# A two-layer hybrid encoder on one core: the order of the first query products, the first loads in halves, and the place of the probabilities' division

## The chip, the cores and the metric

The kernel runs on one core of a Trainium2 chip. The metric is the device time of one execution in microseconds (us). A core has four compute engines that run side by side and meet only at semaphores: TensorE (PE: matrix products; its weight loads are shown apart as PEld), VectorE (DVE), ScalarE (ACT) and GpSimd (POOL), and SyncE (SP), which here issues the loads. Each engine takes its instructions in the order in which they are written, so an instruction that waits holds up all that stand behind it on its engine.

## The reference

The input x has 256 tokens of width 1024. It is normalised once, then passes through two layers:

```
h = layer_norm(x, ln_in_g, ln_in_b)
for i in range(DEPTH):                                   # DEPTH = 2
    z = h @ w_in[i]
    q, k, v, xr, yr, ga, gr = jnp.split(z, split_points, axis=-1)
    ...                                                  # rotary on q, k
    attn = local_attention(q, k, v, attn_sink[i])        # softmax with a sink, 8 heads, 2 kv heads
    ...                                                  # hr: two directions of conv + gated recurrence
    rnn = hr * jax.nn.gelu(yr)
    merged = (jax.nn.sigmoid(ga) * (attn @ w_proj_attn[i])
              + jax.nn.sigmoid(gr) * (rnn @ w_proj_rnn[i]))
    h = layer_norm(DN_ALPHA * h + merged @ w_out[i], ln1_g[i], ln1_b[i])
    ...                                                  # gated MLP with a width-3 conv, per-layer embedding
    h = layer_norm(DN_ALPHA * h + ffn + ple, ln2_g[i], ln2_b[i])
```

All is float32.

## The kernel before

**Three products for one.** TensorE multiplies in a rounded float32 (fp32r). To keep precision each operand is split into a high part (the rounded value) and a low part (what is left), and a product is made of three: high by high, high by low, low by high (the helper three, L522 to L526). The high part of a weight is cast by ScalarE (split_hi, L846 to L850), its low part is made by VectorE as raw minus high (split_lo, L1157 to L1162). The normalised input x is turned by TensorE (turn_rows, L684) into PSUM (misc), from there ScalarE writes x_hi (L864) and VectorE x_lo (L1281), for each tile t of 128 tokens and each half c of the 1024 features.

**Items and homes.** All weights are cut into 168 items of at most 1 MB (ITEMS). An item is loaded by SP into a home: five ordinary ones (W_SLOTS) and two that are buffers of other stages at other times (STATE_HOME, RNN_HOME). The table at L140 to L151 gives each item the home that was used longest ago; where a home had a former item, SP waits until TensorE has used that one (load_item, L450). ScalarE and VectorE split ahead: split_to(l, name, part) splits every item up to the named one plus three.

**The start.** SP loads tile 0 of x, item 0 (first half of the rows of q0), the gains and offsets of the norm (lnp, 1 MB since it is broadcast to all partitions), items 1 and 2, then two small arrays and further items; ScalarE issues the load of tile 1 of x and of the rotary table once tile 0 is there (L1032 to L1034). VectorE takes the statistics of a tile (L1178), the inverse root in small steps (L1188 to L1200), then for each half two passes over 512 columns (L1204, L1207); both passes wait for the whole of lnp (L1201). TensorE turns each half when its norm is done, and begins the query units: q0 and q1 are the 1024 query columns in two units of 512; a unit has two halves hh of the rows, and for every half and token tile token_part (L534) makes 12 products of 512 columns, the three kinds interleaved row block by row block. So the first product waits for the low part of item 0 (s_split, L531) and for x_lo.

**The block loop.** After q0, q1 and xr0 come eight rounds i (WITH_BLOCK, L771): half of a unit of the input projection, one block of the recurrence's gates (gates_block), the other half, and in rounds 3 to 6 turn_probs of attention round r = i - 3, in rounds 2 to 5 the scores of round i - 2. ScalarE makes the exponentials, VectorE the maximum (softmax_max) and the division by the sum (softmax_norm, L1360), whose result turn_probs waits for; it also waits for attn_ready(r), the low part of the attention output of the round before (attn_out, L1367).

## Time and profile before

| | us |
|---|---|
| median of 3 runs | 957.37 (957.37 to 957.76) |
| the profiled execution, its own time | 957.63 |
| its span, first to last instruction | 955.8 |
| TensorE busy | 930.9 (97%) |
| VectorE busy | 725.6 (76%) |
| ScalarE busy | 577.1 (60%) |

All rows below come from the profiled execution. Times are counted from the start of its span. In a timeline a row holds start, duration, engine, line, operation, what it writes and reads, and, in brackets, how long the engine had idled before and what ended that.

### The profile page before, as it was taken

The page shows a single profiled execution, that of the slowest core. Times are in us where ns is not written, and L with a number is a line of the kernel's source. Part 1 is how long each engine was busy: PE and PEld are TensorE (multiplying, and loading weights), DVE is VectorE, ACT ScalarE, POOL GpSimd, SP SyncE. Part 2 cuts the span into 40 slices and gives each one's busy share as a digit, 9 for nine tenths or more (in the row PEclk, how much of TensorE's full clock was granted, in tenths as well). Part 3 has the DMA queues.
Part 4 walks back from the last instruction along what each step waited for, and adds up shares of the span by engine and source line. Part 5 has one row for each costly group of instructions (what it writes and reads, how often), then busy time and mean ns, then how long its engine had stood idle before and what let it go on. Part 6 is the DMA issues. An engine that isn't in the chain of part 4 may idle for free.

```text
span 955.8 us, 12485 instructions
## 1 busy us (share of the span) xinstructions
PE 930.9 (97%) x5068; PEld 801.6 (84%) x5068; DVE 725.6 (76%) x971; ACT 577.1 (60%) x729; POOL 1.5 (0%) x9
## 2 busy tenths in 40 slices
PE   4999999999999999999999999999999999999996
PEld 3898888888888888888889988888888888888885
DVE  6768798697868876867867688887878686866855
ACT  3478889954356654546335889987535555645540
POOL 0000000000000000000000000000000000000000
PEclk9999999999999999999999999999999999999999
DMA  8456435575576556555453645445746755655621
GB/s 312 154 170 204 136 111 164 191 258 204 184 228 203 186 180 203 190 178 197 166 187 113 216 142 174 133 156 196 275 141 219 257 176 187 205 180 185 207 93 44
DMA packets 118040, 174.61 MB, mean 183 GB/s; under 512 B 3936, under 2 KB 78944, under 8 KB 117344
## 3 DMA queue, kind: packets, MB, share of 16 engines
q1 hardware_dynamic: 117696, 173.27, 54.5%
q8 instruction: 40, 0.66, 0.3%
q10 hardware_dynamic: 288, 0.56, 0.2%
q14 instruction: 16, 0.13, 0.0%
HBM read 172.76 MB, written 1.05 MB: 182 GB/s over the span
## 4 chain that ended last, share of the span: by engine, by line
PE 83%; DVE 8%; ACT 7%; issue 1%; DMA 1%; SPq 0%; DVEq 0%; ACTq 0%
PE ring L524 13%; PE ring L526 13%; PE ring L525 13%; PE ring L577 9%; PE ring L573 9%; PE ring L576 5%; PE ring L574 5%; PE misc L524 4%; PE misc L525 4%; PE misc L526 4%; DVE sb_w_lo L1161 2%; ACT sb_w_hi L850 2%; PE misc L682 2%; DVE sb_tmp L1381 1%; ACT sb_soft L943 1%
## 5 line engine op out<-in xcount | busy, mean ns | idle before, releaser
L1161 DVE TENSOR_TENSOR sb_w_lo<-sb_raw,sb_w_hi 128x2048 fp32r<-128x2048 f32 (+1 forms) x140 | 299.6, 2151 | 72.4 <-ACT sb_w_hi L850 72.3
L850 ACT CAST sb_w_hi<-sb_raw 128x2048 fp32r<-128x2048 f32 (+1 forms) x140 | 249.8, 1795 | 19.9 <-DMA sb_raw<-in_w_in_dram 5.0
L524 PE MATMUL ring<-sb_w_hi,sb_x_both 128*128 128x512 f32 x304 | 121.9, 401 | 2.1 <-DVE sb_x_both L1281 2.1
L526 PE MATMUL ring<-sb_w_hi,sb_x_both 128*128 128x512 f32 x304 | 119.4, 393 | 0.0
L525 PE MATMUL ring<-sb_w_lo,sb_x_both 128*128 128x512 f32 x304 | 119.4, 393 | 0.0
L577 PE MATMUL ring<-sb_x_both,sb_w_hi 128*128 128x512 f32 x272 | 107.6, 396 | 0.0
L573 PE MATMUL ring<-sb_x_both,sb_w_hi 128*128 128x512 f32 x272 | 107.5, 395 | 0.0
L576 PE MATMUL ring<-sb_x_both,sb_w_lo 128*128 128x256 f32 x272 | 75.7, 278 | 0.0
L574 PE MATMUL ring<-sb_x_both,sb_w_lo 128*128 128x256 f32 x272 | 75.4, 277 | 0.0
L524 PE MATMUL ring<-sb_x_both,sb_w_hi 128*128 128x256 f32 x256 | 73.0, 285 | 0.0
L525 PE MATMUL ring<-sb_x_both,sb_w_hi 128*128 128x256 f32 x256 | 72.4, 283 | 0.0
L526 PE MATMUL ring<-sb_x_both,sb_w_lo 128*128 128x256 f32 x256 | 72.4, 283 | 0.0
L524 PEld LDWEIGHTS ring<-sb_w_hi,sb_x_both 128*128 128x128 f32 x304 | 57.8, 190 | 14.1 <-DVE sb_x_both L1281 2.7
L526 PEld LDWEIGHTS ring<-sb_w_hi,sb_x_both 128*128 128x128 f32 x304 | 57.6, 190 | 12.5
L525 PEld LDWEIGHTS ring<-sb_w_lo,sb_x_both 128*128 128x128 f32 x304 | 57.9, 190 | 11.4
L968 ACT COPY sb_soft<-ring 128x512 f32<-128x512 f32 x24 | 14.1, 587 | 84.5 <-PE ring L577 84.5
L576 PEld LDWEIGHTS ring<-sb_x_both,sb_w_lo 128*128 128x128 f32 x272 | 51.0, 188 | 12.4
L574 PEld LDWEIGHTS ring<-sb_x_both,sb_w_lo 128*128 128x128 f32 x272 | 51.1, 188 | 11.7
L524 PE MATMUL misc<-sb_w_hi,sb_a_hi 128*128 128x512 f32 x140 | 54.7, 390 | 0.0
L526 PE MATMUL misc<-sb_w_hi,sb_a_lo 128*128 128x512 f32 x140 | 54.5, 389 | 0.0
L525 PE MATMUL misc<-sb_w_lo,sb_a_hi 128*128 128x512 f32 x140 | 54.5, 389 | 0.0
L864 ACT ACTIVATE sb_x_both<-misc 128x512 fp32r<-128x512 f32 x24 | 13.9, 596 | 65.0 <-PE misc L682 65.0
(210 smaller groups left out, 2070.3 us busy)
## 6 DMA issues: line engine op xcount, KB each, us to landing
sb_raw<-in_w_in_dram SPq DMA_DIRECT2D x42, 1024.0 KB, 5.2
sb_raw<-in_w_up_dram SPq DMA_DIRECT2D x34, 1024.0 KB, 5.2
sb_raw<-in_w_down_dram SPq DMA_DIRECT2D x18, 1024.0 KB, 4.9
sb_raw<-in_w_proj_attn_dram SPq DMA_DIRECT2D x8, 1024.0 KB, 5.1
sb_raw<-in_w_proj_rnn_dram SPq DMA_DIRECT2D x8, 1024.0 KB, 5.1
sb_hb<-in_w_up_dram SPq DMA_DIRECT2D x8, 1024.0 KB, 5.3
sb_raw<-in_w_out_dram SPq DMA_DIRECT2D x6, 1024.0 KB, 5.6
sb_raw<-in_w_ple_gate_dram SPq DMA_DIRECT2D x6, 1024.0 KB, 5.6
```

The source lines that it names most:

```text
L524: nc.tensor.matmul(dst, lhs[0], rhs[0], start=first, stop=False)
L525: nc.tensor.matmul(dst, lhs[0], rhs[1], start=False, stop=False)
L526: return nc.tensor.matmul(dst, lhs[1], rhs[0], start=False, stop=last)
L573: nc.tensor.matmul(bank_of(*key), hi[:, cols], x_both[:, k], start=k == 0, stop=False)
L574: nc.tensor.matmul(bank_of(*key)[:, 0:SEQ], lo[:, cols], x_hi[:, k], start=False, stop=False)
L576: nc.tensor.matmul(bank_of(*key)[:, 0:SEQ], lo[:, cols], x_hi[:, k + 1], start=False, stop=False)
L577: last = nc.tensor.matmul(bank_of(*key), hi[:, cols], x_both[:, k + 1], start=False, stop=k + 2 == KT)
L682: return nc.tensor.transpose(dst, src, ident[:])
L850: nc.scalar.copy(hi_at[home][:, 0:size], raw_at[home][:, 0:size]).then_inc(s_hi_part, 1)
L864: nc.scalar.activation(x_hi[:, 4 * c:4 * c + 4, t * P:(t + 1) * P], misc[:, 2 * t + c, :].rearrange("p (k t) -> p k t", k=4), ACT.Copy, sc ...
L968: nc.scalar.copy(half_of(name)[:, hh], ring[:, pair:pair + 2, SEQ:2 * SEQ]).then_inc(s_taken, 1)
L1161: nc.vector.tensor_tensor(lo_at[home][:, 0:size], raw_at[home][:, 0:size], hi_at[home][:, 0:size].bitcast(F32), ALU.subtract).then_inc(s_s ...
```

## The change

It has four parts. (1) In layer 0 the 96 query products are reordered: the 64 whose weight operand is a high part come first, with the turns of x between them, and the 32 with a low part last (first_query_units); layer 1 keeps its order. VectorE no longer splits items 0 and 1 before the norm of tile 1. (2) The first loads: gains and offsets in two halves of 512 columns ahead of the weights, item 0 in two halves with a semaphore each, tile 1 of x issued by SP after them, the rotary table by ScalarE later; ScalarE casts item 0 in two halves. (3) The home table prefers the two shared homes for the first items, so items 0 and 1 lie there, items 2 to 6 in the ordinary ones. Evaluated by hand, the table leaves every FORMER from item 7 on as it was; items 5 and 6, which had to wait for items 0 and 1, wait for nothing. (4) In the block loop of both layers VectorE's softmax_norm moves from behind the gates weight's low part to directly behind the first half's, ahead of attn_out and conv_lo; softmax_max of rounds 1 to 3 moves to the end of the round before, ahead of that round's scan.

```diff
--- before.py
+++ after.py
@@ -140,7 +140,7 @@
 HOME, FORMER, LOADED = [], [], []
 _latest, _loads = {}, [0] * HOMES
 for _n, (_l, _name, _part) in enumerate(ITEMS):
-    _home = min(homes_of(_n), key=lambda home: _latest.get(home, home - HOMES))
+    _home = min(homes_of(_n), key=lambda home: _latest.get(home, home - HOMES * (1 + (home >= W_SLOTS))))
     _former = _latest.get(_home)
     if _home >= W_SLOTS and _n > ITEM[_l, "xr0", 0] and (_former is None or _former < ITEM[_l, "xr0", 0]):
         _former = "state" if _home == STATE_HOME else "rnn"
@@ -153,7 +153,8 @@
 
 def in_pe_order(l):
 
-    steps = [("q0", 0), ("q0", "half"), ("q0", 1), ("q1", "half"), ("q1", 0), ("q1", 1), ("xr0", 0), ("xr0", 1)]
+    steps = [("q0", 0), ("q0", "half"), ("q0", 1)] if l else [("q0", "half"), ("q0", 0), ("q0", 1)]
+    steps += [("q1", "half"), ("q1", 0), ("q1", 1), ("xr0", 0), ("xr0", 1)]
     for i, name in enumerate(WITH_BLOCK):
         feature = UNITS[name][0] == "feature"
         steps += [(name, 0 if feature else "half")]
@@ -471,11 +475,24 @@
                     sp.wait_ge(s_rnn_ready, value("rnn_ready", l, 2))
                 sp.dma_start(lnp[:], a["ln"][bass.ds(2 * l + n, 1)].to_broadcast((P, 2, D))).then_inc(s_lnp, 16)
 
+            def load_first_norm(c, signal):
+
+                at = slice(512 * c, 512 * c + 512)
+                sp.dma_start(lnp[:, :, at], a["ln"][0:1, :, at].to_broadcast((P, 2, 512))).then_inc(signal, 16)
+
             sp.dma_start(h[:, 0, :], a["x"][0, 0:P, :]).then_inc(s_h[0], 16)
+            load_first_norm(0, s_lnp_left)
+            load_first_norm(1, s_lnp)
             for l in range(DEPTH):
                 head = ITEM[l, "q0", 0]
-                load_item(head)
-                load_norm(l, 0)
+                if l == 0:
+                    for i, signal in enumerate((s_raw_first, s_raw[HOME[0]])):
+                        dst = raw_at[HOME[0]][:, 1024 * i:1024 * i + 1024].rearrange("p (k n) -> p k n", k=2)
+                        sp.dma_start(dst, item_source(0)[0][:, 2 * i:2 * i + 2]).then_inc(signal, 16)
+                    sp.dma_start(h[:, 1, :], a["x"][0, P:SEQ, :]).then_inc(s_h[1], 16)
+                else:
+                    load_item(head)
+                    load_norm(l, 0)
                 for n in range(head + 1, head + 3):
                     load_item(n)
                 sp.wait_ge(s_rnn_ready, value("rnn_ready", l, 0))
@@ -678,6 +695,78 @@
                         if (t, c) == (1, 0) and l + 1 < DEPTH:
                             turn_h(l + 1, 0, 0, [1])
 
+            def high_pass(l, name, hh, t, ready, x, ks=range(4)):
+
+                n = ITEM[l, name, hh]
+                hi = hi_at[HOME[n]]
+                if n == 0 and ks[-1] < 2:
+                    pe.wait_ge(s_hi_first, 1)
+                else:
+                    pe.wait_ge(s_hi_part, n + 1)
+                first = hh == 0 and x is x_hi and ks[0] == 0
+                if first:
+                    pe.wait_ge(s_emptied[RING[l, name, t][0]], free(l, name, t))
+                if x is x_hi:
+                    pe.wait_ge(s_x_hi, value("x_hi", l, ready))
+                else:
+                    x_ready(l, ready)
+                for k in ks:
+                    nc.tensor.matmul(bank_of(l, name, t), x[:, 4 * hh + k, t * P:(t + 1) * P],
+                                     hi[:, 512 * k:512 * k + 512], start=first and k == ks[0], stop=False)
+
+            def high_passes(l, name, hh, t, ready):
+                high_pass(l, name, hh, t, ready, x_hi)
+                high_pass(l, name, hh, t, ready, x_lo)
+
+            def low_pass(l, name, hh, t):
+
+                hi, lo = weights(l, name, hh)
+                for k in range(4):
+                    last = nc.tensor.matmul(bank_of(l, name, t), x_hi[:, 4 * hh + k, t * P:(t + 1) * P],
+                                            lo[:, 512 * k:512 * k + 512], start=False, stop=hh == 1 and k == 3)
+                return last
+
+            def first_query_units(l):
+
+                turn_h(l, 0, 0, [0])
+                high_pass(l, "q0", 0, 0, 1, x_hi, range(0, 2))
+                turn_h(l, 0, 0, [1])
+                high_pass(l, "q0", 0, 0, 1, x_lo, range(0, 2))
+                high_pass(l, "q0", 0, 0, 1, x_hi, range(2, 4))
+                high_pass(l, "q0", 0, 0, 1, x_lo, range(2, 4))
+                high_passes(l, "q0", 1, 0, 2)
+                turn_h(l, 0, 1, [0])
+                high_passes(l, "q1", 0, 0, 1)
+                turn_h(l, 0, 1, [1])
+                high_passes(l, "q0", 0, 1, 3)
+                high_passes(l, "q1", 0, 1, 3)
+                high_passes(l, "q0", 1, 1, 4)
+                for t in range(TT):
+                    high_passes(l, "q1", 1, t, 2 + 2 * t)
+                for name in ("q0", "q1"):
+                    low_pass(l, name, 0, 0)
+                    low_pass(l, name, 0, 1).then_inc(s_products, 1)
+                    low_pass(l, name, 1, 0).then_inc(s_products, 1)
+                    low_pass(l, name, 1, 1).then_inc(s_products, 1)
+
...
             def turn(dst, src):
                 return nc.tensor.transpose(dst, src, ident[:])
 
@@ -749,24 +838,9 @@
                 attn = (a_hi, a_lo)
                 rnn = (r_hi, r_lo)
                 if l == 0:
-                    turn_h(l, 0, 0)
-                x_ready(l, 1)
-                token_part(l, "q0", 0, 0, x)
-                x_ready(l, 2)
-                token_part(l, "q0", 1, 0, x).then_inc(s_products, 1)
-                turn_h(l, 0, 1, [0])
-                if l:
-                    token_part(l, "q1", 0, 0, x)
-                turn_h(l, 0, 1, [1])
-                x_ready(l, 3)
-                token_part(l, "q0", 0, 1, x).then_inc(s_products, 1)
-                x_ready(l, 4)
-                token_part(l, "q0", 1, 1, x).then_inc(s_products, 1)
-                if l == 0:
-                    token_part(l, "q1", 0, 0, x)
-                token_part(l, "q1", 0, 1, x).then_inc(s_products, 1)
-                for t in range(TT):
-                    token_part(l, "q1", 1, t, x).then_inc(s_products, 1)
+                    first_query_units(l)
+                else:
+                    query_units(l)
                 feature_unit(l, "xr0")
                 for i, name in enumerate(WITH_BLOCK):
                     half = feature_half if UNITS[name][0] == "feature" else mixer_token_half
@@ -847,7 +921,13 @@
 
                 home, size = HOME[n], item_size(n)
                 act.wait_ge(s_raw[home], LOADED[n])
-                nc.scalar.copy(hi_at[home][:, 0:size], raw_at[home][:, 0:size]).then_inc(s_hi_part, 1)
+                at = slice(1024 if n == 0 else 0, size)
+                nc.scalar.copy(hi_at[home][:, at], raw_at[home][:, at]).then_inc(s_hi_part, 1)
+
+            def split_first_half():
+
+                act.wait_ge(s_raw_first, 16)
+                nc.scalar.copy(hi_at[HOME[0]][:, 0:1024], raw_at[HOME[0]][:, 0:1024]).then_inc(s_hi_first, 1)
 
             split = [0]
 
@@ -1029,16 +1109,20 @@
             def pg_out(l, c, t):
                 out_of(l, f"pg{c}", t, gr[:, t, 512 * c:512 * c + 512], ACT.Tanh, 0.5)
 
-            act.wait_ge(s_h[0], 16)
-            act.dma_start(h[:, 1, :], a["x"][0, P:SEQ, :]).then_inc(s_h[1], 16)
-            act.dma_start(rope[:], a["rope"]).then_inc(s_rope, 16)
             for l in range(DEPTH):
                 if l == 0:
+                    split_first_half()
+                x_parts(l, 0, [(0, 0)], 1.0)
+                if l == 0:
                     split_to(l, "q0", 0, 0)
-                x_parts(l, 0, [(0, 0), (0, 1)], 1.0)
+                x_parts(l, 1, [(0, 1)], 1.0)
                 if l == 0:
                     split_to(l, "q1", 0, 0)
-                x_parts(l, 2, [(1, 0), (1, 1)], 1.0)
+                x_parts(l, 2, [(1, 0)], 1.0)
+                x_parts(l, 3, [(1, 1)], 1.0)
+                if l == 0:
+                    split_to(l, "q1", 1, 0)
+                    act.dma_start(rope[:], a["rope"]).then_inc(s_rope, 16)
                 split_to(l, "q0", 1)
                 unit_out(l, "q0")
                 split_to(l, "q1", 0)
@@ -1198,8 +1282,11 @@
                     norm_step(l, n, t, 5 + 2 * i)
                     nc.vector.scalar_tensor_tensor(out=y, in0=u, scalar=1.5, in1=y, op0=ALU.add,
                                                    op1=ALU.mult).then_inc(s_ln_step, 1)
-                dve.wait_ge(s_lnp, 32 * l + 16 * n + 16)
                 for c in range(2):
+                    if (l, n, t, c) == (0, 0, 0, 0):
+                        dve.wait_ge(s_lnp_left, 16)
+                    else:
+                        dve.wait_ge(s_lnp, 32 * l + 16 * n + 16)
                     at = slice(512 * c, 512 * c + 512)
                     nc.vector.scalar_tensor_tensor(out=h[:, t, at], in0=h[:, t, at], scalar=mean, in1=lnp[:, 0, at],
                                                    op0=ALU.subtract, op1=ALU.mult).then_inc(s_ln_step, 1)
@@ -1506,9 +1593,7 @@
                 add_ffn(l, 0, 1)
                 norm_rest(l, 0, 0)
                 if l == 0:
-                    split_to(l, "q0", 0, 0)
                     x_parts(l, 0, [(0, 0), (0, 1)], 1.0)
-                    split_to(l, "q0", 1, 0)
                     add_ffn(l, 1, 0)
                 else:
                     x_parts(l, 0, [(0, 0)], 1.0)
@@ -1533,22 +1618,20 @@
                 split_to(l, "xr1", 1)
                 conv(l, 2)
                 for i, name in enumerate(WITH_BLOCK[1:], 1):
-                    if 4 <= i <= 6:
-                        softmax_max(l, i - 3)
                     split_to(l, name, 0)
+                    if 3 <= i <= 6:
+                        softmax_norm(l, i - 3)
                     if i >= 4:
                         attn_out(l, i - 4)
                     if i + 1 < 2 * RNN_BLOCKS:
                         conv_lo(l, i + 1)
                     split_to(l, f"rg{i // RNN_BLOCKS}", i % RNN_BLOCKS)
-                    if 3 <= i <= 6:
-                        softmax_norm(l, i - 3)
                     gate_input(l, i)
                     split_to(l, name, 1)
                     if i + 2 < 2 * RNN_BLOCKS:
                         conv(l, i + 2)
-                    if i == 2:
-                        softmax_max(l, 0)
+                    if 2 <= i <= 5:
+                        softmax_max(l, i - 2)
                     if name == "kv":
                         rotate(l)
                     if i % 2 == 1:
```

## Rows read from the trace of the kernel before

**Rows 1.** The page, its parts on busy time and on slices.

```profile
PE 930.9 (97%) x5068; PEld 801.6 (84%) x5068; DVE 725.6 (76%) x971; ACT 577.1 (60%) x729; POOL 1.5 (0%) x9
...
PEclk9999999999999999999999999999999999999999
```

**Rows 2.** Waits of TensorE, whole span: total us, times, longest.

```profile
PE misc L682 <- DVE sb_h L1207: 12.5, 3, 11.8
PE misc L682 <- DVE sb_soft L1360: 2.8, 4, 1.1
```

**Rows 3.** Chain that ended last, first 45 us: start, us, what.

```profile
1.64 8.47 DMA sb_lnp<-in_ln_dram
...
15.99 0.79 PE ring L524
...
21.05 0.43 PE ring L526
...
21.85 0.23 PE ring L525
```

**Rows 4.** Timeline of the start, until x_hi of the first half.

```profile
4.30 1.29 DVE L1178 BATCH_NORM_STATS2 sb_st<-sb_h 128x6 f32<-128x512 f32 x2 [4.30 <-DMA sb_h<-in_x_dram]
...
7.00 1.90 ACT L850 CAST sb_w_hi<-sb_raw 128x2048 fp32r<-128x2048 f32 x1 [0.52 <-DMA sb_raw<-in_w_in_dram]
...
10.14 0.75 DVE L1204 SCALAR_TENSOR_TENSOR sb_h<-sb_h,sb_mv,sb_lnp 128x512 f32<-128x512 f32 x1 [2.59 <-DMA sb_lnp<-in_ln_dram]
...
11.83 1.09 PE L682 MATMUL misc<-sb_ident,sb_h 128*128 128x128 f32 x4 [11.83 <-DVE sb_h L1207]
...
12.95 0.60 ACT L864 ACTIVATE sb_x_both<-misc 128x512 fp32r<-128x512 f32 x1 [4.05 <-PE misc L682]
```

**Rows 5.** Bytes moved, 40 slices of the first 50 us.

```profile
GB/s 0 121 342 395 433 439 419 393 371 376 393 385 241 205 401 392 361 265 28 0 0 0 0 0 110 379 372 360 346 115 39 322 68 0 0 179 376 282 2 31
```

**Rows 6.** Timeline, norm of tile 1 and the last turn of x.

```profile
18.96 1.28 DVE L1178 BATCH_NORM_STATS2 sb_st<-sb_h 128x6 f32<-128x512 f32 x2
...
22.91 0.75 DVE L1207 SCALAR_TENSOR_TENSOR sb_h<-sb_h,sb_mv,sb_lnp 128x512 f32<-128x512 f32 x1
...
25.17 0.66 PE L682 MATMUL misc<-sb_ident,sb_h 128*128 128x128 f32 x4 [0.38 <-DVE sb_h L1207]
...
26.21 0.50 PE L524 MATMUL ring<-sb_w_hi,sb_x_both 128*128 128x512 f32 x1 [0.38 <-DVE sb_x_both L1281]
```

**Rows 7.** Timeline, TensorE's first product of xr0 (256 columns).

```profile
42.66 0.28 PE L524 MATMUL ring<-sb_x_both,sb_w_hi 128*128 128x256 f32 x1
```

**Rows 8.** Timeline of VectorE behind the query stage.

```profile
36.61 0.18 DVE L1300 TENSOR_SCALAR sb_lam_t<-sb_lam_t 128x16 f32<-128x16 f32 x1 [2.40 <-ACT sb_lam_t L1047]
...
50.42 2.46 DVE L1381 SCALAR_TENSOR_TENSOR sb_tmp<-sb_xT,sb_rnnp,sb_tmp 128x255 f32<-128x255 f32 x6 [4.77 <-ACT sb_tmp L883]
```

**Rows 9.** Timeline of TensorE at turn_probs, rounds 4 and 6, layer 0.

```profile
132.55 0.28 PE L526 MATMUL ring<-sb_x_both,sb_w_lo 128*128 128x256 f32 x1
133.88 1.09 PE L682 MATMUL misc<-sb_ident,sb_soft 128*128 128x128 f32 x8 [1.05 <-DVE sb_soft L1360]
...
170.64 1.09 PE L682 MATMUL misc<-sb_ident,sb_soft 128*128 128x128 f32 x8 [0.32 <-DVE sb_soft L1360]
```

**Rows 10.** Timeline of VectorE in round 4, layer 0.

```profile
127.50 2.29 DVE L1161 TENSOR_TENSOR sb_w_lo<-sb_raw,sb_w_hi 128x2048 fp32r<-128x2048 f32 x1
129.70 0.68 DVE L1367 TENSOR_TENSOR sb_a_lo<-misc,sb_a_hi 128x512 fp32r<-128x512 f32 x1
...
132.28 0.15 DVE L1355 TENSOR_TENSOR sb_sm<-sb_sm 128x4 f32<-128x4 f32 x1
...
132.68 1.14 DVE L1360 TENSOR_SCALAR sb_soft<-sb_soft,sb_sm 128x256 f32<-128x256 f32 x4
```

**Rows 11.** Timeline of ScalarE, exponentials of round 4.

```profile
127.62 0.47 ACT L943 ACTIVATE sb_soft<-misc,sb_sm 128x256 f32<-128x256 f32 x1 [1.65 <-DVE sb_sm L1351]
...
129.43 0.21 ACT L946 ACTIVATE sb_sm<-sb_sm 128x4 f32<-128x4 f32 x1
```

More of the change, by code:

```diff
@@ L387, in hybrid_encoder @@
         s_lnp = sem("lnp_loaded")
+        s_lnp_left = sem("first_lnp_left_loaded")
+        s_raw_first = sem("first_raw_half_loaded")
+        s_hi_first = sem("first_hi_half")
         s_small = sem("rnn_params_loaded")
```

16 lines of the change are left out of this document (added).

## The prediction

> **What bounds the kernel now.** I read the page first: TensorE is busy 97% of the span, the next engine 76% [rows 1], so a gain has to come out of TensorE's idle time (955.8 - 930.9 = 24.9 us) or out of products that it makes slowly. The list of waits says where that time is: 12.5 us at the start, nearly all of it before the first turn of x, and 2.8 us in four waits of turn_probs for the division of the probabilities [rows 2]. The few us of the last norm's tail are untouched by this change. The chain of waits then names what ends last at the start: the load of gains and offsets, 8.47 us, and only then norm, turn, low parts and the first product at 15.99 [rows 3]. The timeline shows that VectorE had the inverse root ready and stood idle 2.59 us for that load, until 10.14 [rows 4]. 
>
> Tile 0 of x is still the first load, so the statistics start at 4.30 and the root is ready at 10.14 - 2.59 = 7.55 [rows 4]. Gains and offsets now come second: with x 1.05 MB must have come for the left half, 1.57 MB for the right. The bytes moved (1.25 us a slice) add up to 1.07 MB at 5.0 us and 1.6 MB at 6.2 us [rows 5]. Landings lag that sum: item 0 (1.57 MB in order) was cast at 7.00 [rows 4], 0.8 late. So left lands by about 5.8, right by 7.0, both in time. The wait of 2.59 us goes; the first half's norm ends 2.56 earlier and its turn starts at 11.83 - 2.56 = 9.27, ends at 10.36 [rows 4].
>
> What is late next? The left half of item 0 is now fourth: 2.10 MB, moved by 7.4, landed by 8.2, cast (half of 1.90) by 9.2. It is done before x_hi is wanted at 10.4, with 1.2 to spare. x_hi takes 0.60 and ends at 11.0 [rows 4]. The first product no longer needs a low part of a weight nor x_lo, so it starts at about 11.05 instead of 15.99 [rows 3].
>
> That start is not the gain, since VectorE's norm of tile 1 sets the next point. TensorE makes two products (0.59 for the first up to its successor, 0.43), then the turn of the right half (1.09), which ends at 13.15. x_hi of that half ends at 13.8, x_lo on VectorE at 14.4. Only then do VectorE's statistics of tile 1 start, at 14.4 instead of 18.96 [rows 6]: the two low parts that lay ahead (2.20 each, the pitch of a low part is 129.70 - 127.50 [rows 10]) are moved behind. From the statistics to the left half's norm it took 22.91 + 0.75 - 18.96 = 4.70, so TensorE can turn it at 19.15. Until then TensorE has the other 14 products of q0 for tile 0: from 13.15, six of them to 15.7, then eight, for which ScalarE must have cast item 1 (13.8 to 15.6, loaded by 4.2 MB, that is 13.5). At the lower level they end at 19.1, at the upper at 17.6. Either way TensorE arrives by the time the norm is done; the slow pace is hidden there.
>
> From 19.15: the turn (0.45 at the upper level), eight products of q1 (1.9 with the dearer first one) to 21.5, the turn of the right half to 22.0. Remaining are 40 high products and 32 low ones, 72. Before, 72 products were likewise left at 26.21, the first product behind the last turn [rows 6]; they ended at 42.66 [rows 7], a pitch of 16.45/72 = 0.2285. Nothing should stop them in the new order: x_hi and x_lo of tile 1 are ready while q1 and q0 run; item 3's cast ends by 24.4; the five low parts follow each other on VectorE from 23.1 at 2.2 each and the last of the four that the low products want is ready at 32, wanted only from 36.5. So xr0 begins at 22.0 + 16.45 = 38.45. **Term 1: 42.66 - 38.45 = 4.2 us.**
>
> Does it last? VectorE has as much work as before with TensorE 4.2 us further on. After the fifth low part (34.2) come the small steps of the recurrence's parameters, with a wait for an exponential on ScalarE: before it came at 36.61, after 2.40 of waiting [rows 8]. ScalarE now reads out q0 only at about 35.3, casts item 5 (1.9) and reaches it at 37.3. The steps took 3.0 (36.61 to the next low part); item 5's low part is ready at 42.5. TensorE wants it after xr0's first half, 48 products of 256 columns at 0.12 (5.8): 44.2. Cover 1.7 us; beyond it each us costs one. Further on VectorE stood idle 4.77 before the first conv [rows 8], which covers the 4.2. The homes cost nothing: no former item changes from item 7 on, and items 5 and 6 come earlier. The later rotary table (0.45 us of ScalarE's queue, behind it the cast of item 4) is read far later. SP issues two instructions more and one from ScalarE, all ahead of items that have more than 1 us of cover but item 2: moved by 15.5, landed by about 16.3, cast by 18.2, wanted at 19.6.
>
> **Part 2: the division.** In round 4 TensorE's last product before turn_probs starts at 132.55 and holds 0.12; the turns start at 133.88 [rows 9]. Lost: 1.21, that is the idle 1.05 and 0.16 of modelled tail. Round 6 by the same rule: 0.32 + 0.16 = 0.48 [rows 9]. The second layer repeats both (four waits in all [rows 2]). After the change VectorE, free at 129.70 as before (maximum and scan only swap places ahead of 127.50), makes the division at once: 1.5 us (132.28 to 133.82 [rows 10]), done at 131.3, before 132.67. Its own need, the exponentials, ended at 129.64 after ScalarE had waited 1.65 for the maximum [rows 11]; with the maximum ahead of the scan (3.6 us) ScalarE starts as soon as it is free, 1.65 earlier, and is done at 128.0. What is late next is attn_out, which turn_probs also wants: 129.70 + 1.5 + 0.7 = 131.9, 0.8 before TensorE. conv_lo and the gates weight's low part come 1.5 later, wanted a round later (more than 10 us). The scan ends 2.3 later; nobody waits for it within 3 us. **Term 2: 2 x (1.21 + 0.48) = 3.4 us.**
>
> **The sum.** 957.63 - 4.2 - 3.4 = 950.0 against the profiled execution. That execution is 0.26 above the median of the runs, so the median should be **949.8**.
>
> **A rule against it.** The trace shows the pace change between 21.05 and 21.85 [rows 3], in the middle of a stretch of products without a gap that began at 15.99. By the Trainium skill, "TensorE: Matmul & The Clock Gate", Part 1 and the section on transposes, the gate watches activity freely running against the kernel, and a transpose does not count as busy in the same way. Turns now lie among the first products; by that rule the rise could come late against the first product. This trace can't tell it.
>
> **Rivals.**
> (a) The upper level comes late. Each 512-column product before it costs 0.43 - 0.23 = 0.20 more, a turn of four about 0.5. Up to 19.15 that is hidden, as shown. If the rise stays at 21.3 as in the trace of before [rows 3], half of 19.15 to 21.3 is lost: 1.1 us, 950.9. The same page is where this would come from. If it came at 23, 1.9 us: 951.7. For it: turns and a short gap lie in the way. Against: before, turns at 11.83 and a gap of some us ahead of 15.99 did not prevent a rise before 21.85 [rows 3, 4]. Chance 0.17.
> (b) Term 2 fails: a wait on attn_out or on the exponentials replaces the one on the division. The margins are 0.8 and 1.7. Time 953.2. Chance 0.08.
> (c) Term 1 fails, since the weights arrive later than the bytes say or VectorE is late at item 5 by 1.7 and more; or the new order does not let TensorE start early at all. Time between 950.9 and 954.0 with term 2 whole, 956 if VectorE's lateness also reaches into the block loop. Chance 0.07.
> (d) Slower than before: the division stands ahead of attn_out, and in rounds 4 to 6 VectorE idles there for exponentials that ScalarE makes only behind its own attn_out copy. Price: each us of idle beyond 0.8 is a us of TensorE in six rounds; it outweighs both terms from 0.8 + 7.6/6 = 2.1 us of idle, and at 3 us of it the time is 949.8 + 6 x 2.2 = 963. Round 4 shows 1.7 us of cover instead. Chance 0.03.
>
> **How the numbers follow.** The forecast has 0.65, alone it spans 948.8 to 950.8 (its landings, gaps and turns are good to 0.5 each way, and the pace may rise a little late). The range reaches over (a) and a part of (c): 948.6 to 952.4. About 0.2% (1.9 us) can be told from no change in this kernel. Faster: 0.94, from the forecast, (a), (b), and 0.04 of (c). Same: 0.03, the rest of (c). Slower: 0.03, (d).
>
> **What would show it.** In the profile after: no wait of VectorE for gains and offsets, first turn at 9.3, first product at 11.1; statistics of tile 1 at 14.4; the last turn of x at 21.5; xr0's first product at 38.5 and no idle TensorE between 22 and there; the pace at 0.23 before 19. Rounds 4 and 6 without a wait of turn_probs, in both layers, the division directly behind a low part and ending 1.3 us before the turns. Wrong would be: x_hi waiting behind a cast of item 0, TensorE waiting at s_split for item 5, or turn_probs waiting for L1367.

## The result and the profile after

| | before | after |
|---|---|---|
| median, us | 957.37 | 950.35 (949.98 to 950.9, 4 runs) |
| ratio after to before | | 0.9927 (0.9915 to 0.994) |
| profiled execution, own time | 957.63 | 949.98 |
| its span | 955.8 | 948.2 |
| TensorE busy / idle in the span | 930.9 / 24.9 | 928.1 / 20.1 |

The change makes the kernel 7.0 us faster by the medians; forecast were 7.6. Between the two profiled executions it is 7.65, since that of before lies 0.26 above its median and that of the changed kernel is the fastest of its four.

The waits of TensorE over the whole span of the changed kernel (total us, times, longest); the two rows that answer to [rows 2] are the first, 9.9 for 12.5, and the one that is missing: turn_probs waits for nothing.

```profile
PE misc L771 <- DVE sb_h L1294: 9.9, 2, 9.5
PE ring L714 <- ACT sb_r_hi L925: 1.6, 1, 1.6
PE ring L714 <- ACT sb_x_both L944: 0.8, 1, 0.8
```

The timeline of its start, cut to the steps that the prediction dated (start, duration, engine, line, operation, output and inputs, idle time before and what ended it). They answer to [rows 4], [rows 6] and [rows 7].

```profile
4.62 1.29 DVE L1262 BATCH_NORM_STATS2 sb_st<-sb_h 128x6 f32<-128x512 f32 x2 [4.62 <-DMA sb_h<-in_x_dram]
...
7.80 0.75 DVE L1291 SCALAR_TENSOR_TENSOR sb_h<-sb_h,sb_mv,sb_lnp 128x512 f32<-128x512 f32 x1
...
9.48 1.09 PE L771 MATMUL misc<-sb_ident,sb_h 128*128 128x128 f32 x4 [9.48 <-DVE sb_h L1294]
9.54 1.05 ACT L930 CAST sb_scan_hi<-sb_hb 128x1024 fp32r<-128x1024 f32 x1 [7.52 <-DMA sb_hb<-in_w_in_dram]
...
11.34 1.19 PE L714 MATMUL ring<-sb_scan_hi,sb_x_both 128*128 128x512 f32 x2 [0.78 <-ACT sb_x_both L944]
...
14.66 1.28 DVE L1262 BATCH_NORM_STATS2 sb_st<-sb_h 128x6 f32<-128x512 f32 x2
14.90 1.90 ACT L925 CAST sb_r_hi<-sb_r_raw 128x2048 fp32r<-128x2048 f32 x1 [0.87 <-DMA sb_r_raw<-in_w_in_dram]
...
16.85 2.11 PE L714 MATMUL ring<-sb_r_hi,sb_x_both 128*128 128x512 f32 x8 [1.59 <-ACT sb_r_hi L925]
...
19.42 0.66 PE L771 MATMUL misc<-sb_ident,sb_h 128*128 128x128 f32 x4 [0.46 <-DVE sb_h L1294]
...
38.56 0.28 PE L541 MATMUL ring<-sb_x_both,sb_w_hi 128*128 128x256 f32 x1
```

VectorE no longer waits for gains and offsets: its pass starts at 7.80, as soon as the root is there. The first product comes at 11.34 (15.99 before), tile 1's turn at 19.42, and xr0 at 38.56 instead of 42.66. That is 4.10 us.

At turn_probs, rounds 4 and 6 of layer 0 (to be held against [rows 9]):

```profile
128.38 0.28 PE L543 MATMUL ring<-sb_x_both,sb_w_lo 128*128 128x256 f32 x1
128.50 1.04 PE L771 MATMUL misc<-sb_ident,sb_soft 128*128 128x128 f32 x8
...
164.52 0.40 PE L543 MATMUL ring<-sb_w_hi,sb_x_both 128*128 128x512 f32 x1
164.76 1.04 PE L771 MATMUL misc<-sb_ident,sb_soft 128*128 128x128 f32 x8
```

The turns follow the last product after 0.12 and 0.24, which is that product's own pace. Held against before, TensorE is ahead by 4.10 at xr0, by 133.88 - 128.50 = 5.38 at round 4 and by 170.64 - 164.76 = 5.88 at round 6. So the start gives 4.10, round 4 gives 1.28, round 6 gives 0.50. In layer 1 round 4 stands at 591.12 in the changed kernel and 598.33 before, 7.21 ahead; round 6 at 627.38 and 635.12, 7.74 ahead. Next to nothing is given back behind: the two spans differ by 7.6.

### The profile page after: what moved, and what is told of

The parts are those of the page before. It is cut to its first block, busy times and chain, and to the rows that moved or that the text cites. A ratio compares the mean times of both kernels' runs of the same rounds, so it can differ in the third digit from the quotient of the medians.

```text
span 948.2 us, 12500 instructions
## 1 busy us (share of the span) xinstructions
PE 928.1 (98%) x5068; PEld 800.5 (84%) x5068; DVE 724.2 (76%) x971; ACT 576.6 (61%) x730; POOL 1.4 (0%) x9
## 3 DMA queue, kind: packets, MB, share of 16 engines
HBM read 172.76 MB, written 1.05 MB: 183 GB/s over the span
## 4 chain that ended last, share of the span: by engine, by line
PE 97%; DVE 1%; DMA 1%; ACT 0%; SPq 0%; issue 0%; DVEq 0%
PE ring L541 16%; PE ring L543 16%; PE ring L542 16%; PE ring L594 9%; PE ring L590 9%; PE ring L593 5%; PE ring L591 5%; PE misc L543 5%; PE misc L541 5%; PE misc L542 4%; PE misc L771 2%; PE misc L809 1%; PE misc L829 1%; PE ring L714 1%; DMA sb_hb<-in_w_in_dram 1%; PE ring L725 1%
## 5 line engine op out<-in xcount | busy, mean ns | idle before, releaser
L1245 DVE TENSOR_TENSOR sb_w_lo<-sb_raw,sb_w_hi 128x2048 fp32r<-128x2048 f32 x138 | 294.7, 2148 | 67.5 <-ACT sb_w_hi L925 67.4
L925 ACT CAST sb_w_hi<-sb_raw 128x2048 fp32r<-128x2048 f32 x138 | 246.2, 1795 | 16.1 <-DMA sb_raw<-in_w_proj_rnn_dram 3.9
L541 PE MATMUL ring<-sb_w_hi,sb_x_both 128*128 128x512 f32 x272 | 108.1, 397 | 0.0
L543 PE MATMUL ring<-sb_w_hi,sb_x_both 128*128 128x512 f32 x272 | 106.1, 390 | 0.0
L542 PE MATMUL ring<-sb_w_lo,sb_x_both 128*128 128x512 f32 x272 | 106.0, 390 | 0.0
L543 PEld LDWEIGHTS ring<-sb_w_hi,sb_x_both 128*128 128x128 f32 x272 | 51.1, 188 | 11.0
L541 PEld LDWEIGHTS ring<-sb_w_hi,sb_x_both 128*128 128x128 f32 x272 | 51.1, 188 | 10.0
L542 PEld LDWEIGHTS ring<-sb_w_lo,sb_x_both 128*128 128x128 f32 x272 | 51.2, 188 | 9.9
L590 PEld LDWEIGHTS ring<-sb_x_both,sb_w_hi 128*128 128x128 f32 x272 | 51.6, 190 | 0.3
```

What stands on the lines that cost most here:

```text
L541: nc.tensor.matmul(dst, lhs[0], rhs[0], start=first, stop=False)
L542: nc.tensor.matmul(dst, lhs[0], rhs[1], start=False, stop=False)
L543: return nc.tensor.matmul(dst, lhs[1], rhs[0], start=False, stop=last)
L590: nc.tensor.matmul(bank_of(*key), hi[:, cols], x_both[:, k], start=k == 0, stop=False)
L925: nc.scalar.copy(hi_at[home][:, at], raw_at[home][:, at]).then_inc(s_hi_part, 1)
L1245: nc.vector.tensor_tensor(lo_at[home][:, 0:size], raw_at[home][:, 0:size], hi_at[home][:, 0:size].bitcast(F32), ALU.subtract).then_inc(s_s ...
```

## The experiments

Times below are medians; the kernel before, timed beside each of them, took 957.3 to 957.5. Differences from the changed kernel are taken to its 950.35, whose four runs spread over 0.9 us, so a difference of less than about half a us says nothing by itself; there the traces decide.

### Do the two terms add?

**softmax_only**: the kernel before with the block loop's reordering alone.

```diff
                 for i, name in enumerate(WITH_BLOCK[1:], 1):
-                    if 4 <= i <= 6:
-                        softmax_max(l, i - 3)
                     split_to(l, name, 0)
+                    if 3 <= i <= 6:
+                        softmax_norm(l, i - 3)
                     if i >= 4:
                         attn_out(l, i - 4)
...
-                    if 3 <= i <= 6:
-                        softmax_norm(l, i - 3)
                     gate_input(l, i)
...
-                    if i == 2:
-                        softmax_max(l, 0)
+                    if 2 <= i <= 5:
+                        softmax_max(l, i - 2)
```

> The kernel before with the reordering of maximum and division alone. My theory (two terms that add): turn_probs of rounds 4 and 6 no longer waits in either layer, 3.4 us gained, about 954.0. Rival (the term belongs to the change's start, by which engines meet differently, or a wait on attn_out takes its place): under 1 us gained, 956.5 to 957.4.

Measured: 953.71 (ratio 0.9961, 0.9946 to 0.9976), 3.8 us faster than before. No wait of turn_probs is left. **start_only** is the changed kernel with that same diff undone, so it holds the start and the homes.

> The changed kernel with the old places of maximum and division. Two terms that add: 4.1 us gained, about 953.3, xr0's first product at 38.6, and the four waits of turn_probs back with 1.05 and 0.33 of idle. Rival (shifted engines would have hidden those waits anyway, or the start's gain is given back in the block loop): 950.5 or 955 and more.

Measured: 953.8 (0.9965, 0.9952 to 0.9978), 3.7 us faster than before; the four waits are back:

```profile
PE misc L771 <- DVE sb_soft L1447: 2.7, 4, 1.0
```

3.8 and 3.7 make 7.5, the whole change 7.0: the terms add within what the intervals allow. Its profiled execution took 955.39, its other four 953.77 to 954.02; what happened in it is told below, under the pace.

### Which of the two moves in the block loop?

**division_only**: the changed kernel with the maximum of rounds 1 to 3 back behind the scan.

```diff
                 for i, name in enumerate(WITH_BLOCK[1:], 1):
+                    if 4 <= i <= 6:
+                        softmax_max(l, i - 3)
                     split_to(l, name, 0)
...
-                    if 2 <= i <= 5:
-                        softmax_max(l, i - 2)
+                    if i == 2:
+                        softmax_max(l, 0)
```

> The changed kernel with the division at its new place and the maximum of rounds 1 to 3 back behind the scan. My theory: in round 4 the exponentials end about as VectorE gets to the division, so the division's place is enough: at most 0.5 us slower than the whole change, 950.3 to 950.8. Rival (the earlier maximum is needed, else VectorE idles for the exponentials and attn_out, 0.8 of margin, is late): round 4 or 6 waits by 0.5 or more, 951.5 to 953.

Measured: 950.43 (950.08 to 950.83), the changed kernel's time, and no wait of turn_probs. **maximum_only** leaves the maximum at its new place and puts the division back:

```diff
                     split_to(l, name, 0)
-                    if 3 <= i <= 6:
-                        softmax_norm(l, i - 3)
                     if i >= 4:
...
                     split_to(l, f"rg{i // RNN_BLOCKS}", i % RNN_BLOCKS)
+                    if 3 <= i <= 6:
+                        softmax_norm(l, i - 3)
                     gate_input(l, i)
```

> The changed kernel with the maximum at its new place and the division back behind the gates weight's low part. My theory: the division starts no earlier than before, since VectorE's work ahead of it is the same, so the waits of turn_probs stay: 953.3. Rival (the chain was maximum, exponentials, division, and the maximum opens it): 951 or less.

Measured: 953.23, 2.9 slower than the change. Round 4 of layer 0, from TensorE's timeline:

```profile
129.64 1.09 PE L771 MATMUL misc<-sb_ident,sb_soft 128*128 128x128 f32 x8 [0.80 <-DVE sb_soft L1447]
```

The wait is 0.80 where it was 1.05, and in round 6, where start_only waits 0.31, the list of waits has none any more (two waits, 1.6 us in all, for four and 2.7). From turn to turn TensorE still loses 1.0 in round 4 and 0.3 in round 6 of either layer, where start_only loses 1.2 to 1.3 and 0.5. So the expectation had the time, but its reason, a division that starts no earlier, holds only in the main: alone, the earlier maximum takes some 0.2 us at each of the four turns (953.23 against start_only's 953.8). The division's place takes all of the wait, and beside it the maximum's place is worth nothing (division_only).

### The start: which part carries it?

**loads_only**: the kernel before with the new order of its first loads (item 0 in one piece) and nothing else.

```diff
             sp.dma_start(h[:, 0, :], a["x"][0, 0:P, :]).then_inc(s_h[0], 16)
+            for c, signal in ((0, s_lnp_left), (1, s_lnp)):
+                at = slice(512 * c, 512 * c + 512)
+                sp.dma_start(lnp[:, :, at], a["ln"][0:1, :, at].to_broadcast((P, 2, 512))).then_inc(signal, 16)
...
                 load_item(head)
-                load_norm(l, 0)
+                if l == 0:
+                    sp.dma_start(h[:, 1, :], a["x"][0, P:SEQ, :]).then_inc(s_h[1], 16)
+                else:
+                    load_norm(l, 0)
...
-            act.dma_start(h[:, 1, :], a["x"][0, P:SEQ, :]).then_inc(s_h[1], 16)
...
-                dve.wait_ge(s_lnp, 32 * l + 16 * n + 16)
                 for c in range(2):
+                    if (l, n, t, c) == (0, 0, 0, 0):
+                        dve.wait_ge(s_lnp_left, 16)
+                    else:
+                        dve.wait_ge(s_lnp, 32 * l + 16 * n + 16)
```

> The kernel before with the gains in halves as the first load behind tile 0 of x, item 0 in one piece after them and tile 1 of x then, but the products, the low parts of items 0 and 1 and the places of maximum and division as before. If the order of the loads made the start's gain alone: xr0 at 38.6 and 953.3. My theory, that it needs the products' order too: the norm starts 2.3 earlier, but item 0 lands at about 11.3 and its cast and low part end at 13.2 and 15.4, so the first product starts no earlier than 15.5 to 16.5: 956.6 to 957.9, that is same as before.

Measured: 957.82 (ratio 1.0005, 0.9996 to 1.0014), the same as before. Its timeline shows why:

```profile
9.57 1.09 PE L689 MATMUL misc<-sb_ident,sb_h 128*128 128x128 f32 x4 [9.57 <-DVE sb_h L1216]
...
11.16 1.90 ACT L857 CAST sb_w_hi<-sb_raw 128x2048 fp32r<-128x2048 f32 x1 [4.75 <-DMA sb_raw<-in_w_in_dram]
...
13.10 2.29 DVE L1167 TENSOR_TENSOR sb_w_lo<-sb_raw,sb_w_hi 128x2048 fp32r<-128x2048 f32 x1 [2.22 <-ACT sb_w_hi L857]
...
16.04 0.79 PE L531 MATMUL ring<-sb_w_hi,sb_x_both 128*128 128x512 f32 x1 [4.00 <-DVE sb_x_both L1290]
```

The turn comes 2.3 earlier, but item 0's cast and low part now end at 13.1 and 15.3, and the first product stands at 16.04 (15.99 before [rows 3]). The weight has become what the norm was.

**weights_before_gains**: the changed kernel with item 0 (in halves) loaded ahead of gains and offsets.

```diff
             sp.dma_start(h[:, 0, :], a["x"][0, 0:P, :]).then_inc(s_h[0], 16)
-            load_first_norm(0, s_lnp_left)
-            load_first_norm(1, s_lnp)
...
                         sp.dma_start(dst, item_source(0)[0][:, 2 * i:2 * i + 2]).then_inc(signal, 16)
+                    load_first_norm(0, s_lnp_left)
+                    load_first_norm(1, s_lnp)
```

> The changed kernel with item 0 loaded ahead of gains and offsets, as before (all still in halves). Theory A (the order of the first bytes carries the start): the gains' left half lands at about 8.5 to 9 and the right at 10 to 10.5, the norm of the left half starts 1 to 1.5 us later, the right half's waits too, xr0 at 39.8 to 40.3, 951.5 to 952. Theory B (landings of parts overlap so that their order does not matter, and the reordered products alone make the gain): 950.3 to 950.6.

Measured: 951.82, 1.5 slower than the change; first turn at 10.95, tile 1's turn at 20.89, xr0 at 40.05. Theory A. So of the 4.1 us some 1.5 belong to the loads' order once the products are reordered, and none without that.

**item0_whole**: the changed kernel with item 0 loaded and cast in one piece.

```diff
                 if l == 0:
-                    for i, signal in enumerate((s_raw_first, s_raw[HOME[0]])):
-                        dst = raw_at[HOME[0]][:, 1024 * i:1024 * i + 1024].rearrange("p (k n) -> p k n", k=2)
-                        sp.dma_start(dst, item_source(0)[0][:, 2 * i:2 * i + 2]).then_inc(signal, 16)
+                    load_item(head)
...
                 if l == 0:
-                    split_first_half()
+                    split_to(l, "q0", 0, 0)
                 x_parts(l, 0, [(0, 0)], 1.0)
```

> The changed kernel with item 0 loaded and cast in one piece. Theory A (the halves matter through ScalarE's order): item 0 lands at about 10.9, its cast of 1.9 ends at 12.8 and x_hi waits behind it, the first product comes 2 us later, x_lo of the right half and with it the statistics of tile 1 some 2 us later, xr0 at 40.5, about 952.2. Theory B (the halves are hidden by the wait for tile 1): 950.3 to 950.6.

Measured: 952.02, 1.7 slower. From its timeline:

```profile
11.28 1.90 ACT L920 CAST sb_scan_hi<-sb_hb 128x2048 fp32r<-128x2048 f32 x1 [9.26 <-DMA sb_hb<-in_w_in_dram]
13.09 0.59 ACT L939 ACTIVATE sb_x_both<-misc 128x512 fp32r<-128x512 f32 x1
...
13.82 1.19 PE L709 MATMUL ring<-sb_scan_hi,sb_x_both 128*128 128x512 f32 x2 [3.21 <-ACT sb_x_both L939]
```

x_hi stands behind the whole cast on ScalarE, and everything up to xr0 (41.03) is 2.5 later (its profiled execution, 952.28, is 2.3 slower than that of the changed kernel). Theory A.

**old_homes**: the changed kernel with the old table of homes.

```diff
-    _home = min(homes_of(_n), key=lambda home: _latest.get(home, home - HOMES * (1 + (home >= W_SLOTS))))
+    _home = min(homes_of(_n), key=lambda home: _latest.get(home, home - HOMES))
```

> The changed kernel with the old table of homes, so that items 5 and 6 wait again for the last products of items 0 and 1, which the new order makes late (about 32.6 and 34.5). The prediction costed the homes at nothing, seen as an edit to the kernel before. Theory A (nothing here either): 950.3. Theory B (in the new order they carry weight: item 5 lands at about 37.5, ScalarE's cast of it stands ahead of the exponential of the parameters, VectorE's low part of item 5 comes at about 45.5 to 46, and TensorE waits for it 1.5 to 3 us behind xr0's first half): 952 to 953.5.

Measured: 951.72, 1.4 slower. xr0's first product still stands at 38.62; the loss comes behind it:

```profile
38.44 1.90 ACT L925 CAST sb_w_hi<-sb_raw 128x2048 fp32r<-128x2048 f32 x1 [2.65 <-DMA sb_raw<-in_w_in_dram]
40.24 0.21 ACT L1131 ACTIVATE sb_lam_t<-sb_lam_t 128x16 f32<-128x16 f32 x1
40.49 0.17 DVE L1387 TENSOR_SCALAR sb_lam_t<-sb_lam_t 128x16 f32<-128x16 f32 x1 [5.27 <-ACT sb_lam_t L1131]
...
43.37 5.62 DVE L1245 TENSOR_TENSOR sb_w_lo<-sb_raw,sb_w_hi 128x2048 fp32r<-128x2048 f32 x3
...
45.71 0.39 PE L541 MATMUL ring<-sb_x_both,sb_w_hi 128*128 128x256 f32 x1 [1.18 <-DVE sb_w_lo L1245]
```

Item 5 lands at 38.44, the parameters' exponential stands behind its cast, VectorE waits 5.27 for that, and TensorE waits for item 5's low part. Theory B, a little under its range. The homes bring nothing by themselves, but without them the new order, which frees item 0 only at the end of the query stage, would lose a third of what it wins.

### What stands at the start's end?

**statistics_early**: the changed kernel with VectorE's statistics of tile 1 moved into its idle 2.1 us ahead of x_lo of the right half (layer 0).

```diff
-                if l == 0:
-                    x_parts(l, 0, [(0, 0), (0, 1)], 1.0)
-                    add_ffn(l, 1, 0)
-                else:
-                    x_parts(l, 0, [(0, 0)], 1.0)
-                    add_ffn(l, 1, 0)
-                    x_parts(l, 1, [(0, 1)], 1.0)
-                add_ffn(l, 1, 1)
+                x_parts(l, 0, [(0, 0)], 1.0)
+                add_ffn(l, 1, 0)
+                if l == 0:
+                    add_ffn(l, 1, 1)
+                x_parts(l, 1, [(0, 1)], 1.0)
+                if l:
+                    add_ffn(l, 1, 1)
```

> The changed kernel with VectorE's statistics of tile 1 moved into its idle 2.1 us ahead of x_lo of the right half. Theory A (VectorE's norm of tile 1 alone sets the start): 1.2 us gained over the changed kernel, xr0 at 37.3, 949.1. Theory B (behind it stands the landing of items 1 and 2 with ScalarE's casts, as TensorE is busy with q0 until 18.96 and item 2's cast ends at 19.53): 0.2 to 0.5 us, xr0 at 38.1 to 38.4, 949.8 to 950.1.

Measured: 949.94 (949.74 to 951.22), xr0 at 38.38 in place of 38.56. Theory B, by the trace rather than by the time, since 0.4 us lies inside the spread: tile 1's norm is not alone; right behind it stand the landings of items 1 and 2 (item 2's cast is from 17.68 to 19.6, and the products that want it start at 19.64). Their lateness can be seen in the bytes. The bytes moved in the first 20 us (0.5 us a slice), first of the kernel before, then of the changed one, then of weights_before_gains:

```profile
GB/s 0 0 0 115 188 279 389 373 397 406 422 414 524 426 393 385 434 393 430 389 367 380 351 381 389 393 393 393 381 385 366 203 80 157 308 397 401 403 397 383
```

```profile
GB/s 0 0 0 98 172 336 381 270 233 205 205 295 373 406 406 397 414 410 430 406 406 389 389 389 389 381 389 389 393 393 385 385 360 348 335 324 381 397 389 358
```

```profile
GB/s 0 0 0 115 156 270 393 377 414 410 381 406 385 279 225 205 254 369 414 426 430 422 381 414 401 393 389 389 393 385 389 381 356 332 340 369 406 387 373 365
```

In the changed kernel the rate falls to 205 between 3.5 and 6 us, and where the halves of gains and offsets are loaded later, the dip comes later, from 6.5 to 8.5. Before, with one load for both, there is none in this stretch. **gains_whole** makes it one load again, at its new early place.

```diff
-            load_first_norm(0, s_lnp_left)
-            load_first_norm(1, s_lnp)
+            sp.dma_start(lnp[:], a["ln"][0:1].to_broadcast((P, 2, D))).then_inc(s_lnp, 16)
...
-                    if (l, n, t, c) == (0, 0, 0, 0):
-                        dve.wait_ge(s_lnp_left, 16)
-                    else:
-                        dve.wait_ge(s_lnp, 32 * l + 16 * n + 16)
+                    dve.wait_ge(s_lnp, 32 * l + 16 * n + 16)
```

> The changed kernel with gains and offsets, still the first load behind tile 0 of x, in one load of 4 KB pieces per partition row instead of two of 2 KB pieces. In the changed kernel the bytes moved fall to about 200 to 270 GB/s while the halves move (3.5 to 6 us), and that dip travels with them where they are placed later. Theory A (the halves of 2 KB, all partitions reading the same 2 KB, are what is slow): no dip, 380 or more from 3.5 us on, item 0's left half lands at 8.2 to 8.6 instead of 9.5, item 1 at 13.6 to 13.9 instead of 14.9; the norm is not delayed as the whole lands by 7; TensorE's wait for item 1's cast shrinks from 1.6 to about 0.4; the time stays, 950.1 to 950.4, since tile 1's norm is later. Theory B (the dip comes from the broadcast itself or from the first load's place): the dip stays, the left half's norm waits to about 8, about 951.

Measured: 950.15 (950.04 to 950.16), its bytes:

```profile
GB/s 0 0 0 106 188 344 451 418 442 410 393 360 352 406 401 397 393 434 434 381 422 397 393 389 381 381 389 393 385 389 328 111 79 141 353 393 406 399 397 389
```

The dip is gone. The packets of the stretch from 3.5 to 6 us, first of the changed kernel, then of gains_whole, also show the pieces:

```profile
DMA packets 311, 0.60 MB, mean 242 GB/s; under 512 B 24, under 2 KB 24, under 8 KB 311
```

```profile
DMA packets 144, 1.01 MB, mean 405 GB/s; under 512 B 13, under 2 KB 13, under 8 KB 26
```

The halves moved as packets of 2 KB, while the whole moved as packets of 8 KB (118 of its 144 are not under 8 KB), gains and offsets of a partition together, and not of 4 KB as the expectation has it. The size of the packets alone is not what is slow, for the weights move in packets of 2 KB too, at about 400 (weights_before_gains, the same stretch: 503 packets, 0.99 MB, 397 GB/s).

Item 0's left half is cast from 8.54 (9.54), item 1 from 14.00 without a wait for it (14.90), the wait for item 1's cast has vanished, and the norm's first pass was not held up. The time stays: tile 1's norm (turn at 19.49) is now alone at the end. Theory A.

**gains_whole_statistics_early** is both of these edits.

> Both: gains and offsets in one load, and the statistics of tile 1 ahead of x_lo of the right half. Theory A (landings and tile 1's norm each hide the other): the early statistics now bring what they did not alone, xr0 at 37.4 to 37.7, 949.2. Theory B (the landing is not what holds them): xr0 at 38.3 as with the early statistics alone, 949.9.

Measured: 949.13 (948.75 to 949.42, ratio 0.9914, 0.99 to 0.9927), 1.2 us under the changed kernel, no run of either inside the other's spread; xr0 at 37.84.

```profile
18.75 0.60 PE L765 MATMUL misc<-sb_ident,sb_h 128*128 128x128 f32 x4
19.11 2.10 PE L708 MATMUL ring<-sb_w_hi,sb_x_both 128*128 128x512 f32 x8
...
37.84 0.28 PE L535 MATMUL ring<-sb_x_both,sb_w_hi 128*128 128x256 f32 x1
```

Alone the two edits brought 0.4 and 0.2 by the medians (xr0 0.18 earlier and not earlier at all), together 1.2 (xr0 0.72 earlier): each had been hidden by the other. Held profiled execution against profiled execution, the pair gains 0.85 (949.98 to 949.13), close to xr0's 0.72; the rest of the 1.2 is that the changed kernel's profiled execution was its fastest. Tile 1's turn now stands directly behind the products of q0 at 18.75: TensorE is last there, and the eight products before it still took 2.88 (2.11 in the changed kernel). This is the fastest kernel of the study.

**gains_own_rows**: the changed kernel with the halves read from an array that holds gains and offsets once per partition (the copies are laid out ahead of the launch).

```diff
-                sp.dma_start(lnp[:, :, at], a["ln"][0:1, :, at].to_broadcast((P, 2, 512))).then_inc(signal, 16)
+                sp.dma_start(lnp[:, :, at], a["ln_rows"][:, :, at]).then_inc(signal, 16)
```

> The changed kernel with the halves of gains and offsets read from an array in HBM that holds them once per partition, so in the same 2 KB pieces but each from its own place (the weights, which come in 2 KB pieces from their own places, move at about 390 GB/s). Theory A1 (the slow part is that all partitions read the same 2 KB): no dip, 380 or more, item 0's left half lands by 8.6. Theory A2 (2 KB pieces in this pattern are slow wherever they come from): the dip stays at about 200 to 270, left half at 9.5. Time 950.1 to 950.4 in both.

Measured: 950.03, its profiled execution 951.06. The bytes fall there too, but elsewhere (152 and 184 from 5 to 6 us, 201 at 7 us), and item 0's left half is cast only from 10.75. A1 is wrong, since the rate still breaks in without a shared source. A2 does not fit the place, nor the landing, though that is a weak test: in start_only, whose start is that of the changed kernel, the same cast began at 10.48 in place of 9.54, so executions differ by 0.9 there. Why the halves are slow stays open.

## Why the prediction was right

**The total.** Forecast 950.0 for the profiled execution and 949.8 for the median; measured 949.98 and 950.35. That the first comes within 0.02 is luck: the four runs spread over 0.9 us, and the median is 0.55 off.

**Term 1, forecast 4.2, measured 4.10.** The chain came as dated, each step within 0.3 us up to the last turn: first turn 9.48 (9.27), first product 11.34 (11.05), statistics of tile 1 14.66 (14.4), tile 1's turn 19.42 (19.15), xr0 38.56 (38.45). The step that sets it was named rightly: not the first product, 4.65 earlier, but VectorE's norm of tile 1. Some 0.1 to 0.2 of the 4.10 belongs to the execution of before, in which the pace rose late: softmax_only and loads_only, which keep the old order of products, began xr0 at 42.42 and 42.58. What was off is below it: the landings. Item 0's left half was dated 8.2 and came at 9.5, item 1 13.5 and 14.9, item 2 16.3 and 17.6, because the sum used the rates of [rows 5], in which the gains came as one load, and the halves move at half that: with one load again (gains_whole) the left half is cast from 8.54, which is 1.0 of the 1.3; tile 0 of x itself came 0.3 later than in the trace of before (4.62 for 4.30). The cover stood in the prediction with its sizes: 1.2 us for the left half (used up to the last tenth, its cast ended at 10.59 and x_hi began at 10.60), 1.4 for item 2 (its cast ended at 19.53, wanted at 19.83), and the fourteen products whose end did not matter (TensorE did wait 1.59 for item 1's cast). The error of up to 1.4 us stayed hidden by luck of size: statistics_early shows that with the norm out of the way it is what holds the start.

**The homes, costed at nothing.** As an edit to the kernel before that would be so, but in this change they are a part of term 1: old_homes loses 1.4 us. The prediction had the chain in hand (cast of item 5, exponential, low part, with 1.7 us of cover) and used the homes silently in it. The statement to make was what it costs if that cover goes.

**Term 2, forecast 3.4, measured 1.28 + 0.50 + 1.26 + 0.53 = 3.6** from the steps of TensorE's lead at the four turns (the third from the turns of round 3 in layer 1, at 572.42 and 578.37 before, where the lead is 5.95), and 3.8 from softmax_only, of whose trace 0.24 stands already at xr0. The rule that a wait costs its idle time plus the modelled tail held to 0.1 us in each. Round 4 on VectorE shows the order as dated:

```profile
123.41 2.27 DVE L1245 TENSOR_TENSOR sb_w_lo<-sb_raw,sb_w_hi 128x2048 fp32r<-128x2048 f32 x1
...
126.00 1.14 DVE L1447 TENSOR_SCALAR sb_soft<-sb_soft,sb_sm 128x256 f32<-128x256 f32 x4
127.06 0.68 DVE L1454 TENSOR_TENSOR sb_a_lo<-misc,sb_a_hi 128x512 fp32r<-128x512 f32 x1
```

The division ends at 127.14 and attn_out at 127.74, TensorE arrives at 128.50: 0.76 of cover (0.8 forecast). The prediction gave the earlier maximum a part in this, as the thing that brings the exponentials in time; division_only shows that it is not needed: without it the exponentials come in time too.

**The rivals.** (b) and (d) did not come: there is no idle on VectorE ahead of the division in round 4, and 0.77 us of it in round 5, where attn_out has more than 3 us. (c) came in its first half (late landings) without its price. (a) is the interesting one, and the next section is on it.

## The pace of TensorE in the first products

The products' pace rose at a different point in nearly every profile. In the changed kernel the eight products from 16.85 take 2.11, that is 0.23 each, the 2.4 GHz level, and the six before them, 2.21 in all, are mixed (in start_only's profile the same six, all at the lower pace, take 2.91); the rise falls less than 4 us after the first product. In the profiled execution of start_only, whose start is the same program up to here, it came after 20:

```profile
12.16 1.19 PE L714 MATMUL ring<-sb_scan_hi,sb_x_both 128*128 128x512 f32 x2 [1.35 <-ACT sb_x_both L944]
...
13.86 2.91 PE L714 MATMUL ring<-sb_scan_hi,sb_x_both 128*128 128x512 f32 x6
...
17.78 3.64 PE L714 MATMUL ring<-sb_r_hi,sb_x_both 128*128 128x512 f32 x8 [1.01 <-ACT sb_r_hi L925]
...
21.26 0.60 PE L771 MATMUL misc<-sb_ident,sb_h 128*128 128x128 f32 x4
```

Eight products take 3.64 instead of 2.11, the 1.2 GHz level for nearly all of them. Tile 1's turn stands directly behind them at 21.26: TensorE, not the norm, is now last. xr0 began at 40.36, 1.8 later than in the changed kernel; 0.8 of it was there at the first product already (tile 0 of x and item 0 landed later in that execution), the other 1.0 is the pace: the norm of tile 1 was done at about 20.2. The whole execution took 955.39 where the other four of the same kernel took 953.77 to 954.02. So rival (a) is real: its price was forecast at 1.1 to 1.9, this one execution paid 1.0, and the other four, by their times, did not. Why the rise came late is not shown: the engine's gaps differ too (1.35 and 1.01 before the first and the second group of products, 0.78 and 1.59 in the changed kernel). The granted clock of the page reads full in all of this (1.00 for the first 50 us of the changed kernel). By the Trainium skill ("TensorE: Matmul & The Clock Gate", Part 1) the gate's watch runs free of the kernel, and the point of transition varies by half a us either way for that. That it varies from one execution to the next agrees with the traces; by how much does not, since the two rises here lie more than 4 us apart, counted from the first product.

## What to carry to other kernels

When the engine that sets the time must wait for two chains at its start, find what ends last with each of them taken away, for an edit to one alone can be worth nothing (loads_only) and two edits can be worth more together than the sum of what each brings (gains_whole with statistics_early). Put the part of the work that needs the fewest inputs first, and date each new input's arrival with the pieces in which it will be moved, since a rate read from another cut of the same bytes can be off by two. A consumer's wait for a short step is cured by that step's place in its engine's queue; moving what feeds it helps only where it was late.

## What the runs showed of the hardware

Gains and offsets, 1 MB over all partitions, moved at about 400 GB/s as one broadcast load, in packets of 8 KB, and at 205 to 295 as two loads of 512 columns each, in packets of 2 KB, at two different places in the queue; weights in packets of 2 KB moved at about 400, so the cause isn't settled. TensorE rose from 1.2 to 2.4 GHz less than 4 us after its first product in one execution and more than 8 us after it in another of the same start.
